# Four of eleven down-projection blocks by Strassen's scheme in a two-layer decoder trunk, with the weights' sums on GpSimd

## What is computed

```python
def swiglu(x, w_gu, w_down):
    g, u = jnp.split(x @ w_gu, 2, axis=-1)
    return (jax.nn.silu(g) * u) @ w_down

for i in range(DEPTH):                      # DEPTH = 2, D_MODEL = 1024, D_FF = 2816
    f = swiglu(rms_norm(h, ffn1_pre_g[i]), ffn1_w_gu[i], ffn1_w_down[i])
    h = h + 0.5 * rms_norm(f, ffn1_post_g[i])
    ...
    f = swiglu(rms_norm(h, ffn2_pre_g[i]), ffn2_w_gu[i], ffn2_w_down[i])
    h = h + 0.5 * rms_norm(f, ffn2_post_g[i])
    ...
```

## Time and profile before

| | us |
|---|---|
| median of 3 runs | 1173.55 (1173.36 to 1173.77) |
| the profiled execution | 1174.19, of which the span is 1172.50 |
| PE busy in the span | 1163.0 |
| DVE busy | 858.8 |
| ACT busy | 723.3 |
| POOL busy | 52.0 |

### The profile page before, as it was taken

How to read it: one execution, slowest core, us unless ns; L and a number is a source line. 1 busy time by engine, 2 the same in 40 slices (tenths; PEclk the granted TensorE clock), 3 DMA queues, 4 the chain that set the end, 5 groups by cost and what they waited for, 6 DMA issues and landing times.

```text
span 1172.5 us, 15820 instructions
## 1 busy us (share of the span) xinstructions
PE 1163.0 (99%) x6079; PEld 984.8 (84%) x6079; DVE 858.8 (73%) x1298; ACT 723.3 (62%) x1166; POOL 52.0 (4%) x124
## 2 busy tenths in 40 slices
PE   9999999999999999999999999999999999999997
PEld 7888888888888888888888888888888888888886
DVE  6888846977857888854788887478776678888456
ACT  7666635577755766643686664365776567666345
POOL 4000000000000000000100000010000010000002
PEclk9999999999999999999999999999999999999999
DMA  8666654644354665565556656556535456556550
GB/s 288 218 187 193 221 202 150 226 160 165 112 202 154 187 208 181 182 239 182 178 163 197 190 182 243 193 169 200 172 111 180 157 167 215 180 180 215 199 178 36
DMA packets 138683, 215.77 MB, mean 184 GB/s; under 512 B 6958, under 2 KB 97904, under 8 KB 138608
## 3 DMA queue, kind: packets, MB, share of 16 engines
q1 hardware_dynamic: 135808, 208.43, 54.0%
q10 hardware_dynamic: 2576, 6.29, 1.7%
q0 software_dynamic: 224, 0.04, 0.0%
HBM read 213.68 MB, written 1.05 MB: 183 GB/s over the span
## 4 chain that ended last, share of the span: by engine, by line
PE 98%; DMA 1%; DVE 1%; ACT 0%; issue 0%; POOL 0%; SPq 0%; POOLq 0%; DVEq 0%; ACTq 0%
PE ps L1662 25%; PE ps L1530 17%; PE ps L1532 17%; PE ps L1531 17%; PE ps L1672 13%; PE ps L1882 3%; PE ps L1577 1%; PE ps L1891 1%; DMA raw<-in_w_ple_proj 1%; PE ps L1768 1%; PE ps L1783 1%; PE ps L1742 0%; PE ps L1754 0%; PE ps L1797 0%; DVE w_lo L1076 0%; PE ps L1804 0%
## 5 line engine op out<-in xcount | busy, mean ns | idle before, releaser
L1095 DVE SCALAR_TENSOR_TENSOR w_lo<-raw,g_layer,w_hi 128x512 fp32r<-128x512 f32 (+1 forms) x504 | 356.1, 768 | 86.9 <-ACT w_hi L640 86.9
L640 ACT ACTIVATE w_hi<-raw,g_layer 128x512 fp32r<-128x512 f32 (+1 forms) x524 | 346.4, 732 | 77.6 <-PE ps L1672 47.2
L1662 PE MATMUL ps<-x_both,w_hi 128*128 128x512 f32 x1280 | 313.7, 391 | 0.0
L1662 PEld LDWEIGHTS ps<-x_both,w_hi 128*128 128x128 f32 x1280 | 232.6, 189 | 43.6 <-DVE w_lo L1095 0.3
L1092 DVE TENSOR_TENSOR w_lo<-raw,w_hi 128x1024 fp32r<-128x1024 f32 x114 | 134.8, 1221 | 107.5 <-ACT w_hi L637 107.5
L1530 PE MATMUL ps<-w_hi,x_both 128*128 128x512 f32 x480 | 193.5, 403 | 0.1
L637 ACT ACTIVATE w_hi<-raw 128x1024 fp32r<-128x1024 f32 x114 | 114.6, 1052 | 127.6 <-PE ps L1532 119.2
L1532 PE MATMUL ps<-w_hi,x_both 128*128 128x512 f32 x480 | 187.5, 391 | 0.0
L1531 PE MATMUL ps<-w_lo,x_both 128*128 128x512 f32 x480 | 187.1, 390 | 0.0
L1672 PEld LDWEIGHTS ps<-x_both,w_lo 128*128 128x128 f32 x1280 | 169.6, 191 | 9.3
L1672 PE MATMUL ps<-x_both,w_lo 128*128 128x256 f32 x1280 | 173.2, 283 | 0.0
(11 more groups left out here) (226 smaller groups left out, 1040.9 us busy)
## 6 DMA issues: line engine op xcount, KB each, us to landing
raw<-in_ffn_w_gu SPq DMA_DIRECT2D x170, 512.0 KB, 4.7
raw<-in_ffn_w_down SPq DMA_DIRECT2D x88, 512.0 KB, 4.3
raw<-in_w_in SPq DMA_DIRECT2D x80, 512.0 KB, 4.5
raw<-in_w_out SPq DMA_DIRECT2D x16, 512.0 KB, 4.0
raw<-in_w_ple_gate SPq DMA_DIRECT2D x16, 512.0 KB, 4.1
raw<-in_w_branch_sb SPq DMA_DIRECT2D x8, 512.0 KB, 4.4
raw<-in_w_branch_diff SPq DMA_DIRECT2D x8, 512.0 KB, 4.3
raw<-in_ffn_w_gu SPq DMA_DIRECT2D x12, 256.0 KB, 8.1
```

The lines of the kernel that those rows point to most:

```text
L640: last = act.activation(w_hi[:, s, part], raw[:, s, part], ACT.Copy, scale=g_layer[:, g:g + 1])
L1095: last = dve.scalar_tensor_tensor(out=w_lo[:, s, part], in0=raw[:, s, part], scalar=g_layer[:, g:g + 1], in1=whi[:, part], op0=ALU.mult, o ...
L1662: mm = pe.matmul(dst, w_hi[:, s, cols], x_both[:, :, 4 * half + k, :], start=half == 0 and k == 0, stop=stop and k == 3, skip_group_check= ...
```

## The change

In blocks 1, 3, 5 and 7 of each FFN the block of 256 tokens by 256 channels and the 256 x 1024 weights are taken as 2 x 2 blocks (tokens by channels of 128, weights of 128 x 512). Their product is formed by Strassen's scheme in Winograd's form, with seven products in place of eight. Seven products of three matmuls are 21 matmuls in place of 24.

- **Sums of the chunk, S1 to S4** (128 columns each), are made by DVE in the flat steps: `chunk_sums` and `low_sums`, with `high_sums` on ACT.
- **Sums of the weights, T1 to T4** (512 columns each), are made by GpSimd from `raw` (`weight_sums`), into `tmp`. ACT writes their high parts (`high_t`) and DVE their low parts (`low_t`) into `x_both`, whose former contents are used up when the flat steps have ended. One of the four quarters of the unit itself is no longer split (`high_seven`, `low_seven`).
- **Products.** Four of the seven (M1, M6, M5, M7) stay in banks 4 to 7 over the four blocks. The other three go straight into banks 0 to 2. Behind block 7 ACT copies M1, DVE forms the sums of products (`sum_products`) and adds one of them into each of banks 0 to 3 (`combine`) before blocks 9 and 10 go on in that bank.
- **Rotary angles.** Their two loads and their chain of small ops on GpSimd move from ahead of the first `pre_norm` to behind it.
- The tile `gates` shares its memory with the sums of the chunks. Each unit still raises `split_done` once; in a Strassen block it is `low_t` that does.

```diff
+            def weight_sums(i, f, u0):
+
+                for j in range(S_ALL):
+                    n, u = S_ALL * (2 * i + f) + j, u0 + 2 * NC + SEVEN[j]
+                    b11, b12, b21, b22 = (raw[:, slot(u), q] for q in (B11, B12, B21, B22))
+                    if j:
+                        pool.wait_ge(split_done, UNITS * i + u + SEVEN[j - 1] - SEVEN[j] + 1 + SLOTS)
+                    else:
+                        pool.wait_ge(ht_split, 2 * NC * i + NC * f + SEVEN[-1] + 1)
+                    pool.wait_ge(raw_in[slot(u)], arrived(i, u, 0))
+                    pool.tensor_tensor(t_raw[:, T1], b12, b11, ALU.subtract)
+                    pool.tensor_tensor(t_raw[:, T3], b22, b12, ALU.subtract).then_inc(t_sum, 1)
+                    pool.wait_ge(t_sum, 2 * n + 1)
+                    pool.tensor_tensor(t_raw[:, T2], b22, t_raw[:, T1], ALU.subtract).then_inc(t_step, 1)
+                    pool.wait_ge(t_step, n + 1)
+                    pool.tensor_tensor(t_raw[:, T4], b21, t_raw[:, T2], ALU.subtract).then_inc(t_sum, 1)
...
+            def high_t(i, f, u0, j):
+                n = S_ALL * (2 * i + f) + j
+                before = u0 + 2 * NC + (SEVEN[j - 1] if j else -1)
+                act.wait_ge(units_used, UNITS * i + before + 1 + SLOTS)
+                for half in range(2):
+                    part = slice(half * UNIT // 2, (half + 1) * UNIT // 2)
+                    act.wait_ge(t_sum, 2 * n + half + 1)
+                    act.activation(t_hi[:, part], t_raw[:, part], ACT.Copy).then_inc(t_high, 1)
...
+            def low_t(i, f, j):
+                n = S_ALL * (2 * i + f) + j
+                for half in range(2):
+                    part = slice(half * UNIT // 2, (half + 1) * UNIT // 2)
+                    dve.wait_ge(t_high, 2 * n + half + 1)
+                    last = dve.tensor_tensor(t_lo[:, part], t_raw[:, part], t_hi[:, part].bitcast(F32), ALU.subtract)
+                last.then_inc(split_done, 1)
...
-                for d in range(3, NC):
-                    low(i, u0 + 2 * NC + d)
+                for d in range(3, NC - 2):
+                    if d in SEVEN:
+                        low_seven(i, first + d)
+                        low_t(i, f, SEVEN.index(d))
+                    else:
+                        low(i, first + d)
+                sum_products(i, f, u0)
+                low(i, first + NC - 2)
+                combine(i, f, u0, 0)
+                combine(i, f, u0, 1)
+                low(i, first + NC - 1, halves=(0,))
+                combine(i, f, u0, 2)
+                low(i, first + NC - 1, halves=(1,))
+                combine(i, f, u0, 3)
...
+                def down_seven(d):
+                    u, j = u0 + 2 * NC + d, SEVEN.index(d)
+                    begin(i, u)
+                    pe.wait_ge(ht_split, 2 * NC * i + NC * f + d + 1)
...
+                    products = ((M1_BANK, block(0, 0), weight(B11)), (M6_BANK, summed(S2), turned_sum(T2)),
+                                (M5_BANK, summed(S1), turned_sum(T1)), (M7_BANK, summed(S3), turned_sum(T3)))
+                    for b, x, w in products:
+                        mm = exact(bank(b), *x, *w, first, last)
+                        if last:
+                            mm.then_inc(m_done, 1)
+                    exact(bank(0), *block(1, 0), *weight(B21), False, False)
+                    exact(bank(1), *summed(S4), *weight(B22), False, False)
+                    exact(bank(2), *block(1, 1), *turned_sum(T4), False, False).then_inc(units_used, 1)
```

More of the change, by code:

```diff
@@ L65 @@
 FLAT = NC - 1
+SEVEN = (1, 3, 5, 7)
+S_ALL = len(SEVEN)
 FACTOR = (0.5, 1.0, 0.5, 1.0)
@@ L602, in _ @@
                 pre_norm(i, 2, 12)
+                weight_sums(i, 1, U_FFN2)
                 post_norm(i, 2, 14)
@@ new lines, in low_sums, with low_seven @@
+            def low_sums(i, f, j):
+                dve.wait_ge(s_high, S_ALL * (2 * i + f) + j + 1)
+                dve.tensor_tensor(sums_lo[j], s_raw, sums_hi[j].bitcast(F32), ALU.subtract).then_inc(ht_split, 1)
+            def low_seven(i, u):
+                s = slot(u)
+                for half, part in enumerate((B11, slice(UNIT // 2, UNIT))):
+                    dve.wait_ge(hi_ready, 2 * UNITS * i + 2 * u + half + 1)
+                    dve.tensor_tensor(w_lo[:, s, part], raw[:, s, part], w_hi[:, s, part].bitcast(F32), ALU.subtract)
@@ L1170, in ffn @@
                 low(i, u0 + 3, g0 + 4, halves=(1,))
+                first = u0 + 2 * NC
                 for c in range(1, NC):
-                    low(i, u0 + 2 * c + 2, *g_even(c))
+                    if c - 1 in SEVEN:
+                        chunk_sums(i, f, SEVEN.index(c - 1))
+                    if c < NC - 1:
+                        low(i, u0 + 2 * c + 2, g0)
+                    else:
+                        low(i, first)
                     if c == 1:
@@ L1176, in ffn @@
                         low_ht(i, f, c - 1, glu_u)
-                    low(i, u0 + 2 * c + 3, *g_odd(c))
+                    if c - 1 in SEVEN:
+                        low_sums(i, f, SEVEN.index(c - 1))
+                    if c < NC - 1:
+                        low(i, u0 + 2 * c + 3, g0 + 4)
+                    else:
+                        low_seven(i, first + 1)
                     if c == 1:
@@ L1180, in ffn @@
                     flat_gate(i, f, c)
-                low(i, u0 + 2 * NC + 2)
+                low_t(i, f, 0)
+                low(i, first + 2)
                 low_ht(i, f, NC - 1, glu_u)
@@ L1543, in wide, with deep @@
                 return mm
-            def deep(s, b, xh, xl, k0, t, first, last, before=None, half_done=None):
+            def deep(s, b, xh, xl, k0, t, first, last, before=None, half_done=None, **group):
                 toks = slice(t * P, (t + 1) * P)
@@ L1553, in deep @@
                         mm = exact(bank(b + n), xh[:, k0 + k, toks], xl[:, k0 + k, toks],
-                                   w_hi[:, s, cols], w_lo[:, s, cols], first and k == 0, last and k == 1)
+                                   w_hi[:, s, cols], w_lo[:, s, cols], first and k == 0, last and k == 1, **group)
                     if half_done is not None and (n == 0 or t == 0):
```

176 lines of the change are left out of this document (140 added, 36 removed).

## The result

The changed kernel takes 1176.38 us (median of 13 runs, 1175.55 to 1176.64); the kernel before took 1173.74 us on the same chip (13 runs). The ratio is 1.0022, with a 95% interval of 1.0013 to 1.0030. That is 2.6 us slower: the direction that was forecast, inside its range, and a quarter of the 10.3 us forecast. The profiled execution took 1176.03 us.

What follows compares the result with a forecast made beforehand. PE was taken as the bound, busy 1163.0 of 1172.5 us. Per FFN, 5.3 us of waits less 2.72 gained gave +2.6, four times +10.3: 1183.9 us; range 1162 to 1195, the forecast's own 1176 to 1195.

Steps and rivals of the forecast that it cites:

- PE's gain: Strassen blocks: 21 matmuls for 24 save PE 0.68 us a block, 2.72 an FFN, 10.9 for the kernel.
- The exclusion: Down stages: GpSimd ops reading SBUF and two-SBUF-input DVE ops hold each other off, a turn of 1.1 us per sum.
- Blocks 5 and 7: Down stage: DVE's loop of 10.95 us against PE's 10.20, so PE waits 0.75 us at each.
- Block 3: Down stage: with four turns DVE needs 11.6 us for PE's 10.20, so PE waits 1.4 us.
- Block 1: First Strassen block of a down stage: DVE's low parts end at 146.0, PE wants them at 143.62, waiting 2.4 us.
- standing backlog of 1.8 us: Flat steps: DVE falls 1.8 us behind at the first sums, then neither catches up nor falls further.
- What the flat steps pay: Flat steps: chunk sums cost DVE 1.83 us against 1.96 us of waits; the steps themselves priced at nothing.
- The rotary step: Rotary angles on GpSimd, moved behind the first `pre_norm`: still ready in time, priced at nothing, both ways.
- The end of the stage, the additions, the loads: Blocks 7 to 9: DVE's sums and additions, 5.4 us, are covered; weight loads keep up; all priced at nothing.
- That DVE doesn't wait for GpSimd: Rival in the down stages: all four blocks in time, the whole gain stays, 1162.7 us; 28%.
- turns shorter than 0.98 us: Rival on GpSimd's turns: 0.90 to 0.98 us leaves the kernel within 0.2% (8%), below that say 1169 us (5%).
- by itself fast enough: GpSimd's four weight sums take 5 us against a pair of blocks' 10.20 on PE.

Runs made afterwards that it cites:

- the first experiment: The changed kernel with DVE's two cosine-folding ops moved to the fifth flat step of the first FFN: 1174.17 us, ratio 1.0003 to the kernel before.

## Why the prediction was right and wrong

**PE's gain: right.** 0.68 us a block and 2.72 an FFN were forecast; the kernels with sums of one column or with fills measured 2.74.

**The exclusion: right, both ways.** It was taken at nearly the whole op though no row showed DVE held up, and a turn was put at 1.1 us; no row decided this, and the prediction gave it little better than an even chance (53%). Measured by the distances of starts, DVE's pairs are late by 1.1 (L1177), 2.19 (L1240, two turns) and 1.23 us (L1247): 4.5 us for four, 1.13 each. The estimate of GpSimd's op, 1.24 us, measured 1.28. "SBUF — State Buffer" of the Trainium skill, section "Who interferes with whom", states this lock, and the traces agree: 2.35 us for a pair of DVE's ops beside GpSimd ops that only write, 3.45 beside one that reads. The estimate from a quarter of the figure for 2048 columns in the Trainium skill's "GPSIMD Engine Reference", "Performance versus the Vector engine", was 1.12 us for GpSimd's op; the trace has 1.28.

**Blocks 5 and 7: right to 0.14 us each.** 10.95 us of loop were forecast, 10.81 measured. Two small errors partly cancel here. I had added printed lengths where the ops overlap by some 0.08 us each: by starts the DVE work is 6.28 us, not 6.55, and the turns a little longer. PE's pair takes 10.20, so 0.61 is lost: 0.32 shown as a wait, 0.16 because the start is 0.70 us behind the last for 0.23, and some 0.13 in the next starts.

**Block 3: 1.4 us forecast, 1.07 measured** in FFNs 2 to 4, by the same overlaps: the loop is 11.28 us in the first experiment, for 11.6.

**Block 1: the step that failed.** 2.4 us were forecast, and 0.45 is what is left of FFN 2's 2.74 without the other three. The wrong term is the standing backlog of 1.8 us in "What the flat steps pay". The chunk's sums cost DVE 1.83 us and its two waits of a period hold 1.96, and from this I said that DVE falls 1.8 behind and neither catches up nor falls further. Waits that hold 1.96 us take up 1.83 within the period; 1.8 is the backlog right behind the sums, not at its end. The trace has it back to +0.31 us at 114.88 and to none at 125.59 (0.72 and 0.27 from each kernel's own first down matmul), and the 128-column ops cost less than their length, as they overlap. The timeline of DVE in the changed kernel at these sums:

```profile
107.31 0.29 DVE L1224 TENSOR_TENSOR tmp<-glu 128x128 f32<-128x128 f32 x1
107.51 0.29 DVE L1225 TENSOR_TENSOR tmp<-glu 128x128 f32<-128x128 f32 x1
...
108.16 0.29 DVE L1229 TENSOR_TENSOR tmp<-glu,tmp 128x128 f32<-128x128 f32 x1
108.37 2.07 DVE L1180 SCALAR_TENSOR_TENSOR w_lo<-raw,g_layer,w_hi 128x512 fp32r<-128x512 f32 x3
```

108.37 - 107.31 = 1.06 us for the four, and 1.67 with the 512-column one. With the backlog struck out, DVE would have been forecast at the last L1287 at 137.5 (137.15 measured, in a trace whose down stage also begins 0.41 us earlier), block 1's wait at 0.6 us, and the sum at +0.8 us an FFN, 3.1 in all. No run takes the chunk's sums out by themselves; the backlog is read from these starts. Of the 5.3 us of waits per FFN, 2.74 came: 1.95 of the difference is block 1's, 0.33 block 3's, 0.28 that of blocks 5 and 7. That is 10.2 us over four FFNs, and it would leave the change at nothing, as the first experiment shows (1.0003).

**The rotary step: the second that failed.** "Nothing, both ways" was right for the move of the angles, as the kernel with that move alone shows (1.0001). But I had looked at the GpSimd ops which use the tables and not at the two small DVE ops behind L1212, though one of them stands in the earlier trace rows. They are not in the diff; the change put GpSimd sums beside them. Each waits a turn, `low_seven` with them; worse, ACT's `rope_s` (L1011) waits 7.26 us for L1617 and stands in ACT's order ahead of `high_seven` and `high_t`. The timeline of ACT in the changed kernel:

```profile
151.33 0.26 ACT L1011 ACTIVATE rope_s<-mixed 128x64 f32<-128x64 f32 x1 [7.26 <-DVE mixed L1617]
...
151.78 0.63 ACT L770 ACTIVATE w_hi<-raw 128x512 fp32r<-128x512 f32 x1
...
153.26 1.99 ACT L780 ACTIVATE x_both<-tmp 128x1024 fp32r<-128x1024 f32 x2
```

So block 3 of FFN 1 lost 2.0 us more, which is the 2.2 us that the changed kernel is slower than the first experiment. -10.2 from the mis-sized waits and +2.2 from this take the forecast of +10.3 to +2.3; +2.6 was measured.

**The end of the stage, the additions, the loads: right at nothing.** PE has no wait behind block 7.

**The rivals.** That DVE doesn't wait for GpSimd (28%) is ruled out by the stretched pairs, and its 1162.7 us is what the kernels reach in which GpSimd reads one column or nothing (1162.8). Of turns shorter than 0.98 us nothing is seen either: a turn measured 1.10 to 1.23 us. The expectation of 1203 to 1209 us for six sums failed for the sentence of the prediction that GpSimd is "by itself fast enough": its four ops take 8.4 us of the pair's 10.2, not 5, because each waits for DVE. I had made DVE's side of the turns and left out GpSimd's.

## What to carry to other kernels

Work that reads SBUF on GpSimd was no relief for a DVE that is full of two-input ops. Here each sum held DVE for 1.13 us, while DVE makes the same sum in 0.66, so giving the sums to DVE and placing those of block 1 around its waits turned +2.6 us into -10.5. A backlog is to be followed to the end of the period that holds the waits, not taken as standing. And where an engine gets a new neighbour, list every op of the other engine in that stretch, the small ones and those outside the diff too, and who waits for them.

## What the runs showed of the hardware

- A DVE op of 64 columns with a single input in SBUF (`TENSOR_SCALAR`, float32) waited for a whole GpSimd op: 1.30 us for 0.20 beside a sum, and 0.94 beside a fill that only writes, while DVE's `TENSOR_TENSOR` with two SBUF inputs ran undisturbed beside fills. The Trainium skill's "SBUF — State Buffer", section "Who interferes with whom", has `tensor_scalar` among the ops that can take the shared pair of ports; the two rows agree.
- A waiting GpSimd op got its turn behind a single DVE op, though more were queued: the longest sum took 2.28 us, 1.28 of its own and one DVE op, and with six sums end to end they took 2.05 on average.
- The hold of a DVE pair went by the op's length: 1.1 us for 512 columns, 0.55 for 256.
- PE's restart behind a wait of 0.32 us cost some 0.3 us beyond the wait shown (0.61 in all).
- Behind the wait of 2.73 us in the changed kernel the granted clock stayed at 1.00. With six sums it fell to its lower level, 0.50 (1.2 GHz), during or behind ten of sixteen waits (2.44 to 3.88 us). Behind two waits of 2.60 us it stayed at 1.00, so the length of a wait does not decide it by itself; what does stays open.
